# First products of a hybrid decoder step: one weight slot's pieces cut in halves and interleaved with the transposes of the token rows

## The reference

```python
def rmsnorm(x, g):
    xf = x.astype(jnp.float32)
    y = xf * lax.rsqrt(jnp.mean(xf * xf, axis=-1, keepdims=True) + EPS)
    return (y * g.astype(jnp.float32)).astype(x.dtype)

def rglru_block(xn, h0, conv_buf, w_in, conv_w, conv_b, ...):
    u = xn @ w_in
    gate, xb = u[..., :D_RNN], u[..., D_RNN:]
    xc, new_buf = causal_dwconv(xb, conv_buf, conv_w, conv_b)
    ...
```

## Time and profile before

| | us |
|---|---|
| median of 3 runs (lowest, highest) | 2326.93 (2325.96, 2327.49) |
| the profiled execution, its own time | 2328.91 |
| its span, first to last instruction | 2326.8 |
| PE busy in the span | 2300.0 (99%) |
| DVE, ACT, POOL busy | 1639.5, 1014.2, 1098.3 |

### The profile page before, as it was taken

How to read it: one execution, slowest core, us unless ns; L and a number is a source line. 1 busy time by engine, 2 the same in 40 slices (tenths; PEclk the granted TensorE clock), 3 DMA queues, 4 the chain that set the end, 5 groups by cost and what they waited for, 6 DMA issues and landing times.

```text
span 2326.8 us, 43298 instructions
## 1 busy us (share of the span) xinstructions
PE 2300.0 (99%) x16943; PEld 2243.6 (96%) x16943; DVE 1639.5 (70%) x2172; ACT 1014.2 (44%) x1732; POOL 1098.3 (47%) x922
## 2 busy tenths in 40 slices
PE   9999999999999999999999999999999999999999
PEld 8999999999999999999999867999999999999999
DVE  7666647777777778986466675477777777788962
ACT  6555645333333334433354585453333333344331
POOL 3322466555555555656220153565555555565540
PEclk9999999999999999999999999999999999999999
DMA  4111132222222334322373202222222223254132
GB/s 135 46 46 45 49 101 84 66 73 83 83 72 66 112 103 172 113 79 82 121 102 88 66 19 96 101 67 84 83 83 61 77 83 93 80 186 141 56 103 91
DMA packets 228790, 203.04 MB, mean 87 GB/s; under 512 B 28373, under 2 KB 209821, under 8 KB 228412
## 3 DMA queue, kind: packets, MB, share of 16 engines
q1 hardware_dynamic: 224180, 188.87, 26.2%
q10 hardware_dynamic: 4404, 12.28, 2.2%
q0 software_dynamic: 64, 0.05, 0.0%
HBM read 152.41 MB, written 50.66 MB: 87 GB/s over the span
## 4 chain that ended last, share of the span: by engine, by line
PE 87%; DVE 6%; issue 3%; DMA 2%; ACT 2%; POOL 1%; SPq 0%; ACTq 0%; POOLq 0%; DVEq 0%
PE ps L1461 13%; PE ps L1460 13%; PE ps L1462 13%; PE ps L1218 9%; PE ps L1220 9%; PE ps L1219 9%; PE ps L1480 4%; PE ps L1481 4%; PE ps L1482 4%; PE ps L1701 1%; PE ps L1729 1%; PE ps L1753 1%; DVE later_slots L2983 1%; DMA down_raw<-in_f_w_down 1%; DVE ring L2989 1%
## 5 line engine op out<-in xcount | busy, mean ns | idle before, releaser
L1480 PE MATMUL ps<-ring,later_slots 128*128 128x272 f32 x960 | 279.4, 291 | 6.9 <-DVE later_slots L2983 6.9
L1481 PE MATMUL ps<-ring,later_slots 128*128 128x272 f32 x960 | 277.7, 289 | 0.0
L1482 PE MATMUL ps<-ring,later_slots 128*128 128x272 f32 x960 | 275.8, 287 | 0.0
L2961 DVE SCALAR_TENSOR_TENSOR y<-convin,fcol,y 128x1024 f32<-128x1024 f32 x192 | 227.0, 1222 | 18.8 <-ACT y L2181 17.1
L1461 PE MATMUL ps<-b,slot_a 128*128 128x272 f32 x768 | 221.3, 288 | 0.0
L1460 PE MATMUL ps<-b,slot_a 128*128 128x272 f32 x768 | 221.2, 288 | 0.0
L1462 PE MATMUL ps<-b,slot_a 128*128 128x272 f32 x768 | 220.5, 287 | 0.0
L1480 PEld LDWEIGHTS ps<-ring,later_slots 128*128 128x128 f32 x960 | 182.0, 190 | 9.0 <-DVE later_slots L2983 8.8
L1482 PEld LDWEIGHTS ps<-ring,later_slots 128*128 128x128 f32 x960 | 182.7, 190 | 0.0
L1481 PEld LDWEIGHTS ps<-ring,later_slots 128*128 128x128 f32 x960 | 182.6, 190 | 0.0
L1218 PE MATMUL ps<-sa,whi 128*128 128x384 f32 (+1 forms) x540 | 177.3, 328 | 0.4 <-DVE x L3020 0.3
(11 more groups left out here) (503 smaller groups left out, 7882.6 us busy)
## 6 DMA issues: line engine op xcount, KB each, us to landing
rawu<-in_f_w_up SPq DMA_DIRECT2D x192, 256.0 KB, 4.2
h_spill<-x SPq DMA_DIRECT2D x48, 544.0 KB, 3.1
down_raw<-in_f_w_down SPq DMA_DIRECT2D x48, 384.0 KB, 4.3
part<-h_spill SPq DMA_DIRECT2D x30, 544.0 KB, 5.4
f_spill<-x ACTq DMA_DIRECT2D x16, 544.0 KB, 2.7
x<-f_spill SPq DMA_DIRECT2D x16, 544.0 KB, 8.3
raw<-in_a_w_in SPq DMA_DIRECT2D x16, 512.0 KB, 4.0
last_rows<-h_spill SPq DMA_DIRECT2D x12, 544.0 KB, 4.7
```

Source lines behind the costliest of these rows:

```text
L1480: pe.matmul(out, slot[:, 0, i, :], b_hi, start=(i == 0 and not more), stop=False, skip_group_check=more)
L1481: pe.matmul(out, slot[:, 0, i, :], b_lo, start=False, stop=False, skip_group_check=more)
L1482: last = pe.matmul(out, slot[:, 1, i, :], b_hi, start=False, stop=(i == 2), skip_group_check=more)
L2961: ins = dve.scalar_tensor_tensor(out, g, fcol[:, u, col + t:col + t + 1], out, ALU.mult, ALU.add)
```

## The change

Four places are edited, and no instruction is added or taken away. SP loads slot 1 right behind slot 0, ahead of the token blocks 3 to 5. ACT prepares slot 1 after tile 1 of chunk 0 rather than after tile 7, DVE after tile 2 rather than after tile 7. On PE the two pieces of chunk 0 are cut into parts and laid between the jobs, and `root_spread(1)` and the jobs 12 to 17 move.

```diff
@@ SP
             conv_loads(0, (0,))
+            conv_loads(0, (1,))
             for tt in range(3, 6):
                 token_rows(tt)
-            conv_loads(0, (1,))
@@ PE, first_products
-                set_up(SET_END[0], SET_END[1])
-                for c in range(3):
+                def first_part(s, ks):
+                    if ks[0] == 0:
+                        pe.wait_ge(hi_ready[s], 1)
+                        pe.wait_ge(lo_ready[s], 1)
+                    out = bank(3 * s, 0)
+                    for k in ks:
+                        normed(0)(0, k)
+                        w, hi, lo = ds(k * P, P), split_a[0][k][:, chunk(0)], split_a[1][k][:, chunk(0)]
+                        pe.matmul(out, whi[s][:, w], hi, start=(k == 0), stop=False)
+                        pe.matmul(out, whi[s][:, w], lo, start=False, stop=False)
+                        last = pe.matmul(out, wlo[s][:, w], hi, start=False, stop=(k == KD - 1))
+                    if ks[-1] == KD - 1:
+                        last.then_inc(bank_ready[3 * s], 1)
+
+                pe.wait_ge(tr_act, SET_END[0] // 2)
+                pe.wait_ge(tr_dve, SET_END[0] // 2)
+                first_part(0, (0, 1))
+                set_up(SET_END[0], SET_END[0] + 2)
+                first_part(0, (2, 3))
+                set_up(SET_END[0] + 2, SET_END[0] + 4)
+                first_part(1, (0, 1, 2, 3))
+                set_up(SET_END[0] + 4, SET_END[1])
+                first_part(0, (4, 5, 6, 7))
+                root_spread(1)
+                first_part(1, (4, 5, 6, 7))
+                set_up(SET_END[1], SET_END[2] - 2)
+                for c in range(1, 3):
                     for s in range(2):
-                        if c == 0:
-                            pe.wait_ge(hi_ready[s], 1)
-                            pe.wait_ge(lo_ready[s], 1)
...
                             if (c, k) == (1, KD - 2):
                                 root_spread(2)
+                            elif (c, k) == (1, KD - 4):
+                                set_up(SET_END[2] - 2, SET_END[2])
...
-                        if (c, s) == (0, 0):
-                            root_spread(1)
-                            set_up(SET_END[1], SET_END[2] - 2)
-                        elif (c, s) == (0, 1):
-                            set_up(SET_END[2] - 2, SET_END[2])
-                        elif (c, s) == (1, 1):
+                        if (c, s) == (1, 1):
@@ ACT, first_chunk_in
                 elif k == 7:
+                    set_up(SET_END[0] + 2, SET_END[1])
+                if k == 1:
                     prep(0, 1, KD * P)
-                    set_up(SET_END[0] + 2, SET_END[1])
@@ DVE, first_chunk_in
                 elif k == 3:
                     set_up(SET_END[0], SET_END[0] + 2)
+                elif k == 2:
+                    prep(0, 1, KD * P)
                 elif k == 7:
                     row_inverse(1)
                     set_up(SET_END[0] + 2, SET_END[1])
-                    prep(0, 1, KD * P)
```

## The result

| | before | changed |
|---|---|---|
| median of 20 runs, us | 2327.22 | 2330.96 |
| profiled execution, us (span) | 2328.91 (2326.8) | 2330.84 (2328.7) |
| granted TensorE clock over the span | 0.995 | 0.995 |

The ratio of the run times is 1.0014, 95% interval 1.0008 to 1.0021: 1.9 to 4.9 us slower, 3.3 in the middle. The forecast was 2330.3, 3.4 us slower. One of the changed kernel's 20 runs took 12789.08 us, a disturbed one that the ratio leaves out.

A forecast was written before the change was run, and what follows sets the result against it. Bound at the beginning by PE's order and each chunk's chain start: +3.1 us for chunk 1's later start and +0.3 for the clock give +3.4, 2330.3 us. Range 2327.3 to 2332.3; main case 2329.3 to 2331.5, chance 0.60.

The forecast's parts named there:

- What is bound: Up to 24 us: PE's order and each chunk's chain start bind; PE's waits before 17.00 total 4.0 us.
- Load order: Block 3 behind slot 1 lands at about 12.5 us instead of 11.05; ACT's squares start 0.2 later, the rest hidden.
- The first tiles and job 6: PE's first matmul at 13.7 us, tile 1 done at 15.1; ACT's copy of job 6 moves from 14.66 to 15.75.
- Slot 1 early: On DVE the 1.21 us of `wlo[1]` move ahead of tile 4's normalization, from 15.33 to 17.1, 1.8 us later.
- POOL beside DVE: POOL's tile 3 low part starts inside `wlo[1]` and ends at 18.2 us; without contention the sum is 0.35 smaller.
- PE from tile 3 on: PE works 6.4 us from 18.2 to the second spread at 24.6; DVE starts chunk 1 3.1 us later.
- The clock: PE's 3.1 us wait likely halves the clock at about 13 us, costing +0.65; 0.3 taken, between 0 and 0.65.
- The sum: Whole kernel: +3.1 us for chunk 1's later start and +0.3 for the clock make +3.4, 2330.3 us, slower by 0.15%.
- Rival (a): Half clock on PE reaches the dense part from 18.2 us: +4.7 to +5.5, 2331.7 to 2332.4 us; chance 0.17.
- Rival (b): Early products count, second spread done before 22.35 us: 2326.0, or 2322.9 with chunk 1's chain earlier; chance 0.07.
- Rival (c): Chain shortened: copies done before chunk 1, no POOL collision, block 3 early; +1 to +2.3, 2328 to 2329.3 us; chance 0.16.
- What there was to recover: PE's idle times before 17.00 us, 4.0 us or 0.17%, were held to be all that could be recovered.

The follow-up runs named there:

- e1: Changed kernel with the second root_spread on PE moved ahead of tiles 4 to 7 of slot 0; ratio 1.0016, frow 41.95 us after the first spread.
- e2: Changed kernel with second root_spread ahead of slot 0's tiles 4 to 7 and jobs 12 to 15 ahead of slot 1's; ratio 1.0010, frow at 40.21 us.
- e3: Changed kernel with 26 more transposes, results unused, on PE in the wait behind the first spread; ratio 1.0024, frow 41.30 us after the first spread.
- e6: Changed kernel with jobs 6 and 7 put back ahead of tiles 0 and 1 of slot 0; frow 41.68 us after the first spread, no ratio.
- e4: Kernel before with only the edits of SP, ACT and DVE, PE's order untouched; ratio 1.0009, frow 39.08 us after the first spread.
- e9: Changed kernel with the edits of e2 and e3 together; ratio 1.0016, frow 39.02 us after the first spread.
- e8: Kernel of e7 with `wlo` of slot 1 made by POOL instead of DVE; ratio to before 0.9990, frow 38.28 us after the first spread.
- e10: Same program as e8, profiled and timed once more; ratio to before 0.9999, frow 38.29 us after the first spread.
- e7: Kernel before, on PE second root_spread ahead of tile 7 of piece (0, 0), first parameter-transpose job inside piece (1, 1); ratio 0.9998, frow at 36.72 us.
- e5: Changed kernel's PE order, but slot 1 loaded and prepared late, the SP, ACT and DVE edits undone; frow 48.81 us after the first spread, no ratio.

## Why the prediction was right

- *What is bound.* Right: the waits ahead of 17 us were not what limits; the chain of each chunk is. PE's first matmul moved from 17.00 to 13.57, and the end of the stretch moved 3.9 us the other way.
- *Load order.* Block 3 was estimated at 12.5 (11.0 to 13.0) and was there at 13.09, just past the upper end. It was not hidden on ACT, which waited 1.04 us for it, nor on DVE, which then waited 1.34 us for tile 2's rounding; it was hidden from the second spread, because tile 3 waited longer still for job 6. In e1 and e2 ACT began the squares 0.8 to 1.1 us sooner after the first spread and PE's tile 3 came at 9.45 and 9.63, against 9.58. e3 and e6 show that block 3 counts when job 6 does not.
- *The first tiles and job 6.* First matmul 13.57 (13.7 forecast); the copy of job 6 at 16.68 (15.75, and 16.7 with the clock at half); tile 3's rounding at 17.17 (16.2, 17.15 with half clock). This is the step that makes the first 2.23 us. e6 moves just this, but there block 3 took over as the limit.
- *Slot 1 early.* Tile 4 at 17.31 (17.1 forecast). In the changed kernel `wlo` of slot 1 was done at 17.40, 0.43 us ahead of POOL's tile 3, and so not on the path to the second spread. e4's 1.27 us are the price of the three edits in PE's old order.
- *POOL beside DVE.* The mechanism is shown by e3 and e4, but it cost nothing in the changed kernel itself: with the clock at half, POOL's tile 3 began at 17.83, when `wlo` (16.18 + 1.22) was done, and took 1.00. The 0.35 us that the sum gave it belonged to the case of full clock only, as the prediction's 0.3 won back says.
- *PE from tile 3 on.* 6.4 us forecast to the second spread; 25.43 - 18.88 = 6.55 measured. DVE's idle time ahead of chunk 1 is 2.07 us (over 2 forecast). e2 shows that this order costs 1.86 us of the 2.03; e1 corrects the name of the step: not the spread alone, the jobs 12 and 13 as well.
- *Chunk 1.* PE waits for POOL inside the piece (1, 0), 0.63 + 0.78 = 1.4 us (2 forecast).
- *The clock.* The term that was mis-sized. It fell at 13 us and was back before 17, as forecast. e3 prices it at 0.77 us (about 0.5 with block 3 as late as in the changed kernel) and e9 against e2 at 1.19, with block 3 early; the prediction had worked out 0.65 for a fall and then took 0.3, as a weight between falling and not. Rival (a), half clock in the dense part, did not come in this kernel's profile, but e2, e8 and e10 had it at half until 18.2, 19.3 and 20.7 us, so it can happen in this stretch.
- *The sum.* 3.4 us forecast, 3.3 (1.9 to 4.9) by the run times, 4.26 by the marks. The mechanism is the forecast one: with the full 0.65 for the clock the prediction puts chunk 1 at 26.15, and it started at 26.30. That the sum meets the middle of the run times to 0.1 us is partly luck, as the marks moved by 0.9 more and the run times leave 3 us of room. Rival (b) is refuted by the profile, where the second spread starts at 25.43 and would have had to be done before 22.35. Rival (c), 1 to 2.3 us, overlaps the interval of the run times, but the marks exclude it.
- *What there was to recover.* Wrong, though nothing in the sum rests on it: the prediction held the 4.0 us ahead of 17 us for all there is. e7 moved frow by 1.09 us by two moves behind 17 us, in waits of ACT and DVE that PE feels only in short gaps.

The parts, then: of the 2.03 us of work ahead of the spread, e2 gives back 1.86. Of the 2.23 us by which tile 3 is late, the clock is 0.5 to 1.2, as block 3 comes late or early, and 1.06 are left in e9, where the clock was full. These hang on the place of the jobs 6 and 7 behind the tiles 0 and 1. Putting the jobs back alone does not win them: e6 won 0.39, as it met the late block 3 and `wlo` of slot 1 beside POOL.

The profiled spans differ by 1.9 us only, not 3.9. The shift can be followed by waits that both traces have, here before the FFN's down projections, the row of before and the row of the changed kernel:

```profile
877.82 0.39 PE L1480 MATMUL ps<-ring,first_slots 128*128 128x272 f32 x1 [1.41 <-DVE first_slots L2983]
```
```profile
882.36 0.39 PE L1499 MATMUL ps<-ring,first_slots 128*128 128x272 f32 x1 [1.40 <-DVE first_slots L3004]
```

It is 4.54 us there. Between 1382 and 1442 us the kernel before had the clock at half longer; two windows of it and the same of the changed kernel:

```profile
1382.00:1392.00 10.00, 10.00 (x67) 0.66 0.00 0
1432.00:1442.00 10.00, 10.00 (x83) 0.66 0.93 332
```
```profile
1382.00:1392.00 10.00, 10.00 (x104) 0.83 0.01 2
1432.00:1442.00 10.00, 10.00 (x101) 1.00 0.81 293
```

These windows hold (0.83 + 1.00 - 0.66 - 0.66) x 10 = 5.1 us of full-speed clock more in the changed kernel. In the windows 1530 to 1540 and 1560 to 1570 it is the other way round: 0.83 in both in the changed kernel and 1.00 before, 3.4 us less. At 2050 us the same kind of wait (2048.62 before, 2050.53 changed) is 1.9 us apart. So half-clock stretches far behind take some of the shift away again, but the figures do not close (4.54 - 5.1 + 3.4 = 2.8, not 1.9); the rest is not assigned, and that the change has no part in these stretches is likely and not shown.

## What to carry to other kernels

Work put into a queue's idle time is not free when a short link of another engine's chain stands behind it: ask not only whether the queue has room, but which of its instructions someone waits for next, and keep those ahead of bulk work. Here there were three: the jobs 6 and 7, the second spread, and the jobs 12 and 13. Moving one such link (e1) does nothing if the next link (the jobs 12 and 13) is still behind the same bulk. A wait that is cut up and moved can come back as one longer wait, with the clock on top. And two costs of equal size need not be one cost: e4's 1.27 us and e9's 1.21 us look alike and lie on different paths.

## What the runs showed that I had not expected

- POOL and DVE: when a low part on POOL began during a `wlo` of DVE (two SBUF inputs), it ended 0.85 us after DVE's end, whether it had begun 0.50, 0.76 or 1.12 us before that end: in e3 at 17.83 against 16.98, in e4 at 17.79 against 16.94, before at 14.53 against 13.67, 0.86. Alone it takes 1.00. The Trainium skill, GPSIMD Engine Reference, section 1 (Specifications), names contention of the two engines when VectorE reads two inputs from SBUF; the trace agrees, and by these rows POOL gets hardly anywhere until DVE is done.
- The half clock falls at different places in executions of one stretch of work. In the changed kernel there was one at 1534 us and one at 1566 us, where the kernel before had none, and the long ones of before at 1383 and 1434 us were short or missing. e8 and e10, the same program, had theirs in the first piece 1.4 us apart. Nor does the same wait always bring it: each of the twelve traces has a wait of PE of 2.74 to 2.76 us that ends between 884 and 897 us, and the clock fell to half around it in six of them (before, changed, e2, e5, e7, e8) and not in the other six. The profiled spans reached from 2325.5 (e4, e7) to 2335.3 us (e5) while marks at 50 us explain only part of it: e3 had the longest span but one, 2333.8, with a better mark than the changed kernel.
- Block 3's landing, with the same order of loads, let ACT start its squares at 12.16 (e9), 12.66 (e3), 13.09 (changed) and 13.47 us (e6): 1.3 us of scatter in what a fixed order gives.
